# Two token-mixing blocks on one Trainium2 core: three row products done as three fp32r products each

## The reference, cut to what matters

```python
# first block, end of the token mix
mix = concatenate([ret_lat, rwkv_lat], axis=-1) @ w_out          # 1024x1024 @ 1024x1024
x = x + gt1 * rms_norm(mix, g_post_mix)
h2 = rms_norm(x, g_pre_ffn) * (1.0 + sc2) + sh2                  # feeds the experts of block 1
...
# second block
x = x + mixed @ w_out_2                                          # 1024x1024 @ 1024x1024
x = x + memory_cross_attention(...)                              # ends in o @ w_co, 1024x512 @ 512x1024
x = x + hierarchical_moe(rms_norm_2(x, norm_ffn), ...)
```

## Time and profile before

| | |
|---|---|
| time before, median of 3 runs | 5133.84 us (5125.55 to 5133.88) |
| profiled execution: its time, its span | 5133.01 us, 5131.2 us |
| mean granted TensorE clock | 0.906 |
| TensorE products busy | 4263.7 us (83%) |
| TensorE weight loads busy | 2915.1 us (57%) |
| VectorE, ScalarE, GpSimd busy | 2338.6 us (46%), 1681.4 us (33%), 408.2 us (8%) |
| DMA | 845.81 MB, 165 GB/s mean |

### The profile page before, as it was taken

The page is one execution under the profiler, slowest core; times in us unless marked ns, Lnnn a source line. Parts: engine busy times, 40 slices in busy tenths (PEclk is TensorE's granted clock), DMA queues, the critical chain, the costliest instruction groups (busy, mean ns, idle before and its releaser), DMA issues. The chain is left out here.

```text
span 5131.2 us, 73014 instructions
## 1 busy us (share of the span) xinstructions
PE 4263.7 (83%) x29841; PEld 2915.1 (57%) x29841; DVE 2338.6 (46%) x3821; ACT 1681.4 (33%) x3170; POOL 408.2 (8%) x376
## 2 busy tenths in 40 slices
PE   4999976868886838999759999877789987499995
PEld 1788844458884316676547444756533454266663
DVE  2211155566664356566441564226600244366664
ACT  2211023545553105444231343126610132144442
POOL 0000012210003000000000230000000000100001
PEclk6999976979998869999979999988989998699998
DMA  6222131552223329999642321221021223599997
GB/s 243 93 85 88 63 120 54 171 156 81 78 78 128 127 80 365 368 363 369 235 169 85 116 97 68 103 96 50 25 90 52 87 58 119 231 363 384 385 381 288
DMA packets 416991, 845.81 MB, mean 165 GB/s; under 512 B 35520, under 2 KB 236256, under 8 KB 413336
## 3 DMA queue, kind: packets, MB, share of 16 engines
q1 hardware_dynamic: 396184, 782.68, 42.5%
q0 software_dynamic: 12032, 41.96, 2.6%
q10 hardware_dynamic: 8448, 16.56, 1.0%
HBM read 676.74 MB, written 164.36 MB: 164 GB/s over the span
## 5 line engine op out<-in xcount | busy, mean ns | idle before, releaser
L390 PE MATMUL psum<-proj_hi,proj_w 128*128 128x512 f32 (+2 forms) x1728 | 460.7, 355 | 15.1 <-DVE proj_w L430 13.0
L2610 PE MATMUL psum<-qkv_w,hT 128*128 128x512 f32 x768 | 336.1, 596 | 12.6 <-DMA qkv_w<-in_w_in 12.6
L2402 ACT ACTIVATE moe_hi<-moe_raw 128x2048 fp32r<-128x2048 f32 x128 | 244.9, 1917 | 302.4 <-PE psum L2353 255.5
L390 PEld LDWEIGHTS psum<-proj_hi,proj_w 128*128 128x128 f32 (+1 forms) x1728 | 303.8, 188 | 65.3 <-DVE proj_w L430 13.4
L2437 DVE TENSOR_TENSOR moe_lo<-moe_raw,moe_hi 128x2048 fp32r<-128x2048 f32 x128 | 291.2, 2288 | 89.1 <-ACT moe_hi L2402 87.5
L390 PE MATMUL psum<-proj_lo,proj_w 128*128 128x512 f32 (+2 forms) x864 | 306.1, 354 | 0.0
L3978 DVE TENSOR_TENSOR moe_lo<-moe_raw,moe_hi 128x2048 fp32r<-128x2048 f32 x128 | 287.0, 2284 | 33.8 <-ACT moe_hi L3944 33.8
L2610 PEld LDWEIGHTS psum<-qkv_w,hT 128*128 128x128 f32 x768 | 145.7, 191 | 190.5 <-issue 177.1
L3944 ACT ACTIVATE moe_hi<-moe_raw 128x2048 fp32r<-128x2048 f32 x128 | 236.6, 1904 | 7.4 <-DMA moe_raw<-in_w_gate_up 7.2
L3198 PE MATMUL psum<-branches_T,mixed_w 128*128 128x512 f32 x512 | 222.8, 598 | 13.8 <-DMA mixed_w<-in_w_attn_o 13.8
L2363 PE MATMUL psum<-moe_wd,moe_hidT 128*128 128x512 f32 x512 | 224.6, 597 | 8.6 <-DVE moe_hidT L2458 8.6
(11 more groups left out here) (594 smaller groups left out, 8547.6 us busy)
## 6 DMA issues: line engine op xcount, KB each, us to landing
moe_raw<-in_w_gate_up SPq DMA_DIRECT2D x128, 1024.0 KB, 16.2
moe_raw<-in_w_gate SPq DMA_DIRECT2D x64, 1024.0 KB, 7.0
moe_raw<-in_w_up SPq DMA_DIRECT2D x64, 1024.0 KB, 7.4
moe_wd<-in_w_down SPq DMA_DIRECT2D x64, 1024.0 KB, 9.3
moe_wd<-in_w_down SPq DMA_DIRECT2D x32, 2048.0 KB, 10.9
mod_w<-in_w_mod SPq DMA_DIRECT2D x24, 1024.0 KB, 13.9
uT<-proj_out SPq DMA_DIRECT2D x35, 640.0 KB, 2.9
chunks_pr<-prim SPq DMA_DIRECT2D x40, 512.0 KB, 4.1
```

What stands on the lines that cost most here:

```text
L390: ins = nc.tensor.matmul(bank[e * nch + c][0:width, 0:n], l, r, start=(k == 0 and i == 0), stop=(k == KD - 1 and i == 2))
L2402: nc.scalar.activation(hi[:, n % R], raw[:, n % R], ACT.Copy).then_inc(s["hi_ready"], 1)
L2610: last = nc.tensor.matmul(bank[2 * (n % 2) + c_][:, :], hT[:, k, i * P:(i + 1) * P], w[:, m % 2, k, c_ * BANK:(c_ + 1) * BANK], start=(k = ...
```

## The change

The weights and the token tiles are each split into a leading part, rounded to fp32r (a copy on ScalarE), and the rest (on VectorE, the value minus the leading part, again fp32r). A product of 128x128 by 128x512 then becomes three products: leading by leading, leading tokens by rest of weights, rest of tokens by leading weights; rest by rest is left out. For that `wt` holds two parts, `xs_hi` and `xs_lo` hold two token tiles each, and a buffer `room` of four slices takes the raw weights; the same buffer later serves as `ht`, `yt` and `sq2`.

Loads are now whole slices of 128x1024, four at first and the others one by one as `room` comes free. TensorE begins slice by slice, on tiles 0 and 1 by turns: two slices of tile 0, one of tile 1, and so on; then the last half of tile 1, and then the transposes of tile 0. Each slice goes into both column halves. The edit is the same for the three stages. The number of semaphores in a stage goes from 29 to 35.

```diff
     KK = K // P
...
     with Stage(nc, name) as st:
-        wt = st.sb("w", [P, KK, D])
+        wt = st.sb("w", [P, 2, KK, D], F32R)
+        xs_hi, xs_lo = st.sb("xs_hi", [P, 2, KK, P], F32R), st.sb("xs_lo", [P, 2, KK, P], F32R)
+        room = st.sb("room", [P, 4, D])
+        ht, yt, sq2 = room[:, 0:2, :], room[:, 2, :], room[:, 3, :]
         xt = st.sb("x", [P, 4, D])
...
         ss = st.sb("ss", [P, NT, 5])
-        gb, yt = st.sb("g", [P, D]), st.sb("y", [P, D])
-        w_in, g_in, x_in = [st.sem(f"w_in{c}") for c in range(2)], st.sem("g_in"), [st.sem(f"x_in{i}") for i in range(4)]
+        gb = st.sb("g", [P, D])
+        w_in, g_in, x_in = [st.sem(f"w_in{r}") for r in range(4)], st.sem("g_in"), [st.sem(f"x_in{i}") for i in range(4)]
         mm, ssq, ms, root, rstd, scaled, out_ready = (st.sem(n) for n in
...
         stored = [st.sem(f"stored{i}") for i in range(4)]
-        sq2 = st.sb("sq2", [P, D])
-        ht, hg = st.sb("h", [P, 2, D]), st.sb("hg", [P, per, D])
+        w_hi, w_lo, x_hi, x_lo = (st.sem(n) for n in ("w_hi", "w_lo", "x_hi", "x_lo"))
+        hg = st.sb("hg", [P, per, D])
         hs = st.sb("hs", [P, NT, 4])
...
         ident = cst[:, CONST["ident"]:CONST["ident"] + P]
-        WIN = 16 * (KK - len(exchanged) + 2 * len(exchanged))
+        landed = [16 * sum(2 if j in exchanged else 1 for j in range(k % 4, k + 1, 4)) for k in range(KK)]
         with nc.Block() as block:
...
             def _(sp):
-                for c in range(2):
-                    cc = slice(c * BANK, (c + 1) * BANK)
-                    for k in range(KK):
-                        if k in exchanged:
-                            for h in range(2):
-                                sp.dma_start(wt[64 * h:64 * h + 64, k, cc],
-                                             w[k * P + 64 * (1 - h):k * P + 64 * (1 - h) + 64, cc]).then_inc(w_in[c], 16)
-                        else:
-                            sp.dma_start(wt[:, k, cc], w[k * P:(k + 1) * P, cc]).then_inc(w_in[c], 16)
-                    if c == 0 and grow is not None:
-                        sp.dma_start(gb[:, :], grow.partition_broadcast(P).rearrange("p o d -> p (o d)")).then_inc(g_in, 16)
+                def load(k):
+                    if k >= 4:
+                        sp.wait_ge(w_lo, k - 3)
+                    if k in exchanged:
+                        for h in range(2):
+                            sp.dma_start(room[64 * h:64 * h + 64, k % 4, :],
+                                         w[k * P + 64 * (1 - h):k * P + 64 * (1 - h) + 64, :]).then_inc(w_in[k % 4], 16)
+                    else:
+                        sp.dma_start(room[:, k % 4, :], w[k * P:(k + 1) * P, :]).then_inc(w_in[k % 4], 16)
+                for k in range(4):
+                    load(k)
+                if grow is not None:
+                    sp.dma_start(gb[:, :], grow.partition_broadcast(P).rearrange("p o d -> p (o d)")).then_inc(g_in, 16)
+                for k in range(4, KK):
+                    load(k)
                 for i in range(4):
...
                 for i, row in enumerate(h_rows or ()):
...
                                                   ht[:, i % 2, k * P:(k + 1) * P], ident)
...
-                for i in range(NT):
-                    for c in range(2):
-                        if i == 0:
-                            pe.wait_ge(w_in[c], WIN)
-                        if i >= 2 and c == 0:
-                            pe.wait_ge(scaled if grow is not None else out_ready, 2 * (i - 1))
-                        for k in range(KK):
-                            last = nc.tensor.matmul(bank[2 * (i % 2) + c][:, :], actT[:, k, i * P:(i + 1) * P],
-                                                    wt[:, k, c * BANK:(c + 1) * BANK], start=(k == 0), stop=(k == KK - 1))
-                        last.then_inc(mm, 1)
-                    if i:
-                        turn(i - 1)
+                def slice_of(i, k):
+                    if i == 0:
+                        pe.wait_ge(w_lo, k + 1)
+                    for n, (l, r) in enumerate(((xs_hi, 0), (xs_hi, 1), (xs_lo, 0))):
+                        for c in range(2):
+                            last = nc.tensor.matmul(bank[2 * (i % 2) + c][:, :], l[:, i % 2, k, :],
+                                                    wt[:, r, k, c * BANK:(c + 1) * BANK],
+                                                    start=(k == 0 and n == 0), stop=(k == KK - 1 and n == 2))
+                            if k == KK - 1 and n == 2:
+                                last.then_inc(mm, 1)
+                pe.wait_ge(x_lo, 1)
+                for k in range(0, KK, 2):
+                    slice_of(0, k)
+                    slice_of(0, k + 1)
+                    if k == 0:
+                        pe.wait_ge(x_lo, 2)
+                    slice_of(1, k // 2)
+                for k in range(KK // 2, KK):
+                    slice_of(1, k)
+                turn(0)
+                for i in range(2, NT):
+                    pe.wait_ge(x_lo, i + 1)
+                    pe.wait_ge(scaled if grow is not None else out_ready, 2 * (i - 1))
+                    for k in range(KK):
+                        slice_of(i, k)
+                    turn(i - 1)
                 turn(NT - 1)
             def evacuate(eng, e, i):
...
             def _(act):
+                def leading(i):
+                    if i >= 2:
+                        act.wait_ge(mm, 2 * (i - 1))
+                    nc.scalar.activation(xs_hi[:, i % 2, :, :], actT[:, :, i * P:(i + 1) * P], ACT.Copy).then_inc(x_hi, 1)
+                for k in range(KK):
+                    if k < 2:
+                        leading(k)
+                    act.wait_ge(w_in[k % 4], landed[k])
+                    nc.scalar.activation(wt[:, 0, k, :], room[:, k % 4, :], ACT.Copy).then_inc(w_hi, 1)
                 for i in range(NT + 2):
...
                         j = i - 1
...
                                 act.wait_ge(ssq, 2 * i + c)
...
                                                  accum_out=ss[:, i, c:c + 1]).then_inc(ssq, 1)
+                    if i + 2 < NT:
+                        leading(i + 2)
+                    if i < NT and grow is not None:
                         act.wait_ge(ms, i + 1)
...
             def _(dve):
+                def rest(i):
+                    dve.wait_ge(x_hi, i + 1)
+                    nc.vector.tensor_tensor(xs_lo[:, i % 2, :, :], actT[:, :, i * P:(i + 1) * P], xs_hi[:, i % 2, :, :],
+                                            ALU.subtract).then_inc(x_lo, 1)
+                for k in range(KK):
+                    if k < 2:
+                        rest(k)
+                    dve.wait_ge(w_hi, k + 1)
+                    nc.vector.tensor_tensor(wt[:, 1, k, :], room[:, k % 4, :], wt[:, 0, k, :], ALU.subtract).then_inc(w_lo, 1)
                 def norm(i):
...
                     nc.vector.tensor_scalar(hs[:, i, 1:2], hs[:, i, 0:1], 1.0 / D, EPS, ALU.mult, ALU.add).then_inc(hms, 1)
...
                             dve.wait_ge(mm, 2 * i + c + 1)
...
                                 .then_inc(out_ready, 1)
+                    if i + 2 < NT:
+                        rest(i + 2)
...
```

## The result

The changed kernel takes 5072.11 us, the median of 4 runs (5069.44 to 5078.46), against 5133.86 us for the kernel before (median of 4 runs on the same chip): a ratio of 0.9885, with a 95% interval of 0.9868 to 0.9902. It is faster by 61.7 us. Forecast were 5079 us, in a range from 5069 to 5091.

The account below looks back on a forecast made before the run. TensorE's float32 products, 0.858 us each, were taken to bound the three stages. Savings of 21.9 (`mix`), 23.8 (`out2`) and 9.5 us (`co`), less 1.0 for semaphores, took 54.2 off 5133.0: 5079 us, range 5069 to 5091.

Parts of the forecast that it names:

- Steady tiles: Three fp32r products at 0.2267 us each make a tile 11.76 us in place of 14.60, in `co` 6.32 for 7.74.
- faster products: Rival: products take the 216 ns of the isolated gap, giving 5069 us; chance 0.03.
- no effect: Rival: splits make three products take one float32 product's time, 0.286 us each, so only the start gains; chance 0.02.
- The start: Each stage's first product comes 6.0 us after its first load; later loads and splits stay behind the products.
- rival of a slow feed: The first slice lands later than 3.6 us; at twice the landing time 11 us more, 5090; chance 0.08.
- The clock at the start: TensorE begins each stage at the low clock; half the low time is lost, 2.5 us (1.7 to 3.1).
- rival of a clock kept low through both tiles: Products begun in pieces keep 1.2 GHz through both first tiles, 18 + 18 + 8 us: 5123; rival's chance 0.06.
- The rival that ended slower: TensorE is granted 1.2 GHz for the fp32r stream, 192 us more: 5271; chance 0.03.
- The wait behind tile 1: Tile 0's transposes wait once for normed rows: 3.5 us plus 2.5 of lost clock in `mix`, 1.7 in `co`.
- rival of the norm chain: In `mix` the chain grows from 10.3 to 13 us and six tiles lose 1.3 each: 5087; chance 0.05.
- The tails: Stage ends lengthen: 0.8 us in `mix`, 0.7 in `out2` and `co`; clearing six more semaphores each costs 1 us in all.
- The 0.9 us for `out2`'s last transposes at the low clock: In `out2` the idle stretch grows from 2.5 to 3.2 us, so the last transposes go low: +0.9 us.

Follow-up runs that it names:

- four_products: The change with a fourth product, rest by rest, added: 5138.51 us in one run, beside 5133.65 for the kernel before.
- two_slots: The change with two slots of `room` for raw weight slices in place of four: 5083.07 us in one run.
- one_tile: The change without turns between tiles 0 and 1: tile 0 slice by slice, tile 1 whole, then tile 0's transposes; 5074.79 us in one run.
- late_turn: The change with the transposes of tile 0 moved from behind tile 1 to the middle of tile 2: 5068.75 us in one run.
- start_only: The kernel before with the start by slices on tiles 0 and 1 by turns, float32 products, nothing split: 5103.68 us, ratio 0.9964.
- after_again: The changed kernel, no edit, run and profiled a second time: 5064.43 us, ratio 0.9877 to the kernel before.
- products_only: The change with its start undone: TensorE waits until all weight slices are split, then takes tile 0 and tile 1 whole; 5094.89 us, ratio 0.9945.

## Why the prediction was right, point by point

**Steady tiles: right.** Three products of one slice and two column halves follow each other like this in `mix`:

```profile
1699.43 1.07 PE L2023 MATMUL psum<-mix_w,mix_xs_hi 128*128 128x512 f32 x4
...
1700.79 1.07 PE L2023 MATMUL psum<-mix_w,mix_xs_hi 128*128 128x512 f32 x4
```

Six products in 1.36 us are 0.2267 us each, the value taken from the projections. four_products has the same price by another way. With it fall the rivals of faster products and of no effect. The Trainium skill's 216 ns ("TensorE: Matmul & The Clock Gate", Back-to-back issue gap) are not reached, here as in the projections.

**The start: right in its sum, its feed mis-sized.** The first product came after 6.2 us in place of 6.0. But the splits of slices 4 to 7 were done 15.7, 17.9, 20.2 and 22.3 us after the first load, not 12.0, 14.4, 15.7 and 17.0. Their rows in `mix`:

```profile
1692.09 5.93 SPq L1974 DMA_DIRECT2D mix_room<-in_w_out  x8
...
1699.37 1.06 ACT L2074 ACTIVATE mix_w<-mix_room 128x1024 fp32r<-128x1024 f32 x1 [4.17 <-DMA mix_room<-in_w_out]
1700.47 1.23 DVE L2110 TENSOR_TENSOR mix_w<-mix_room,mix_w 128x1024 fp32r<-128x1024 f32 x1 [3.86 <-ACT mix_w L2074]
...
1703.98 1.20 PE L2023 MATMUL psum<-mix_w,mix_xs_hi 128*128 128x512 f32 x4 [0.30 <-DVE mix_w L2110]
...
1707.03 1.23 DVE L2110 TENSOR_TENSOR mix_w<-mix_room,mix_w 128x1024 fp32r<-128x1024 f32 x1 [0.82 <-ACT mix_w L2074]
1708.31 1.20 PE L2023 MATMUL psum<-mix_w,mix_xs_hi 128*128 128x512 f32 x4
```

The first of these slices, in two loads of 64 rows, was used 7.3 us after its first issue, where the prediction had 3.6 for a whole slice. Its sentence that a doubled load "would still be ready (20.6)" was the weak one: the slices come one behind the other, 2.2 us apart, and the last is ready 0.05 us before its product. TensorE reaches slice 7 at 22.3 us; the forecast had a margin of 5 us where there is none. The idle time is 0.3 us, but from start to start the six products at slice 5 took 1.96 us (1703.06 to 1705.02) and the six at slice 7 took 1.59 (1707.76 to 1709.35), where 1.36 each would do: 0.8 us lost. The rival of a slow feed put the delay at the first slice, which was not late (3.75 us); the delay came behind it, where it is nearly free. two_slots shows what lies beyond.

**The clock at the start: right in kind and size.** A window over the first 3 us of products in `mix`, and one over what follows (compare):

```profile
1692.30:1695.30 3.00, 3.00 (x7) 2.35 (x8) 3.00 (x3) 2.51 (x3) 0.00 (x0) 0.50 1.06 325
1695.30:1718.00 22.70, 21.18 (x90) 16.51 (x88) 11.80 (x16) 9.13 (x17) 0.00 (x0) 0.99 0.80 241
```

TensorE runs at 1.2 GHz at first, then at 2.4 GHz, although it is handed its work piece by piece. So the rival of a clock kept low through both tiles falls. The granted clock was 0.50 for the first 3.5, 5.7 and 5.4 us of products in `mix`, `out2` and `co`, which costs half of that, 1.8, 2.8 and 2.7 us, where 2.5 were charged for each. In `mix` the 0.7 us saved here and the 0.8 us lost by the feed nearly cancel, and tile 1 was done 30.8 us after the first load in place of 30.3; that this sum came out so well is luck. The Trainium skill (the same page, Loop structure matters more than you think) warns of transfers waited for ahead of each group of products. The waits of the change (0.3 us once) and of one_tile (0.5 to 0.7 us four times) cost no clock; two_slots agrees with the warning, as its wait of 2.22 us for a slice was followed by a granted clock of 0.50. The rival that ended slower, the low clock for the whole stream, falls by the rows above.

**The wait behind tile 1: right in place and kind.** 2.84 us in place of 3.5, as the normed rows were ready 9.6 us after tile 0's last product ended (1709.97 to 1719.57), not 10.3; 1.36 in `co` in place of 1.7, none in `out2`. It comes once a stage and never in a steady tile, so the rival of the norm chain falls. From tile 0's transposes to tile 1's lie 13.48 us, 1.7 more than between steady tiles: that is what the clock cost, where 2.5 us were charged. late_turn, which has neither, gains 5.0 us against 2.84 + 1.7 = 4.5.

**The tails: right in sum, one part wrong.** From the last transposes in `mix` to the next load it was 5.46 us (1821.37 to 1826.83) and is 5.84 us (1801.47 to 1807.31), so that six more semaphores cost 0.38 us a stage, 1.1 in all, as charged. start_only bears this out: its `mix` has the same 35 semaphores and the same 5.84 us, its `co` has 31 and takes 5.60 us, where 29 took 5.46 and 35 took 5.83. The 0.9 us for `out2`'s last transposes at the low clock did not come: they took 1.09 us after 2.93 us of waiting. In other executions they took up to 1.75 us after the same wait (last section), so this term could not be read from one row. For `mix`, 0.56 us of 0.8 came.

**What was not in the sum.** The saving forecast was 54.2 us, the profiled pair gives 62.8: 1.7 us of the difference are in the three stages, 6.9 in unchanged ones. The attention stage accounts for 7.4 us between the two profiles, and its two lengths do not follow the kernel. The medians of the runs saved 61.7 and 58.2 us in the two comparisons, against 55.9 and 55.3 in the stages of the profiled pairs, so a small effect of the change on other stages is not excluded; no run tried it.

## What to carry to other kernels

Where float32 products set the time, three fp32r products of split operands are worth what the same kind takes elsewhere in the same trace (0.2267 against 0.858 us for a 128x512 product), if the stage can begin before the last slice is split; without the start by slices 24.9 of the 55.9 us were gone. Ask of each tile's follow-up work what it waits for when the tiles ahead end closer together: here moving one call by half a tile gave 6.2 to 7.5 us more (against after_again and after), while the two-tile order gave nothing. For a change of 1%, read the stages that it touches by their own first and last rows, since the rest of the program moved by about 20 us (4758.5 to 4779.2) between executions.

## What the runs showed of the hardware

How long TensorE's first work takes after a wait does not tell whether the clock was lost. The change waited 2.84 us and its eight transposes took 1.97 us; after_again waited 2.87 us and they took 1.09:

```profile
1716.58 1.09 PE L2013 MATMUL psum<-cst,mix_room 128*128 128x128 f32 x8 [2.87 <-DVE mix_room L2131]
...
1730.04 1.03 PE L2013 MATMUL psum<-cst,mix_room 128*128 128x128 f32 x8
```

By the transposes alone it looks as if the clock was kept. But the next transposes follow after 13.46 us, as in the change (13.48), and the windows of after_again (the clock is the third number from the end) show where it went:

```profile
1716.50:1717.60 1.10, 1.02 (x9) 1.02 (x10) 0.76 (x5) 0.20 (x1) 0.00 (x0) 1.00 0.24 97
1717.60:1718.60 1.00, 1.00 (x5) 0.77 (x4) 1.00 (x2) 0.00 (x0) 0.00 (x0) 0.57 1.04 369
1718.60:1720.00 1.40, 1.40 (x5) 1.11 (x4) 1.33 (x3) 0.05 (x1) 0.00 (x0) 0.50 0.92 296
1720.00:1722.00 2.00, 2.00 (x8) 1.57 (x7) 1.70 (x4) 1.78 (x4) 0.00 (x0) 0.71 0.83 338
1722.00:1730.00 8.00, 8.00 (x37) 6.57 (x36) 2.86 (x3) 0.01 (x1) 0.00 (x0) 1.00 0.38 132
```

The granted clock was 1.00 through the transposes and fell to 0.50 about 1 us after the wait's end, while TensorE was fully busy. After a wait of 1.36 us (`co`) it did not fall, nor after the 1.94 us in two_slots; after the 2.22 us there it did. So the 1.09 us that the earlier trace rows have after 2.50 us of waiting, which the prediction read as a clock kept, say nothing of what products behind them would have met; there are none there. The last transposes of `out2` show how little their length tells. After the same 2.93 us of waiting they took 1.09 us in the change, after_again, products_only and two_slots, 1.31 in late_turn, 1.50 in four_products and 1.75 in one_tile. After 2.50 us they took 1.09 us before and 1.97 in start_only. So the two rows of before (1.09 us after 2.50, 1.97 after 3.03) set no limit between them, as the prediction had taken them to. What decides when it falls was not tried.
